# A first mixer whose suffix sums move from TensorE to VectorE, and a packed level of distance 32 in the third

## What is computed

```
log_keep = where(strict, log_sigmoid(-z), 0)
suffix   = reverse cumsum of log_keep over the keys, without the element itself
a        = where(strict, exp(log_sigmoid(z) + suffix), 0)
o        = a @ v
```

## Time and profile before

| | |
|---|---|
| median of 3 runs | 1150.33 us (1150.04 to 1150.42) |
| the profiled execution, its own time | 1150.12 us |
| its span in the trace | 1148.6 us |
| PE busy | 1127.5 us (98%) |
| VectorE busy | 552.2 us (48%) |
| ScalarE busy | 251.0 us (22%) |
| GpSimd busy | 21.6 us (2%) |
| mean granted TensorE clock | 0.998 of 2.4 GHz |

### The profile page before, as it was taken

How to read it: one execution, slowest core, us unless ns; L and a number is a source line. 1 busy time by engine, 2 the same in 40 slices (tenths; PEclk the granted TensorE clock), 3 DMA queues, 4 the chain that set the end, 5 groups by cost and what they waited for, 6 DMA issues and landing times.

```text
span 1148.6 us, 13943 instructions
## 1 busy us (share of the span) xinstructions
PE 1127.5 (98%) x5717; PEld 965.0 (84%) x5717; DVE 552.2 (48%) x1084; ACT 251.0 (22%) x470; POOL 21.6 (2%) x83
## 2 busy tenths in 40 slices
PE   7899999999999999999999999999999999999997
PEld 5688888888888877888888888888889888888886
DVE  2455646455465658553646546567463341221123
ACT  3322223000000045663300000007333410000001
POOL 1000230000000000000000000000000000000000
PEclk9999999999999999999999999999999999999999
DMA  9899718787886762380878688664341544353521
GB/s 350 275 368 323 251 50 311 276 311 245 312 279 243 224 74 74 107 259 2 312 279 301 233 313 284 240 235 130 130 142 41 165 147 147 128 198 114 168 89 37
DMA packets 154592, 234.54 MB, mean 204 GB/s; under 512 B 8817, under 2 KB 126625, under 8 KB 154529
## 3 DMA queue, kind: packets, MB, share of 16 engines
q1 hardware_dynamic: 154172, 233.54, 60.1%
q10 hardware_dynamic: 357, 0.12, 0.0%
HBM read 232.19 MB, written 1.44 MB: 203 GB/s over the span
## 4 chain that ended last, share of the span: by engine, by line
PE 93%; DVE 3%; SPq 1%; ACT 1%; DMA 1%; issue 0%; DVEq 0%
PE PS L687 48%; PE PS L764 20%; PE PS L715 7%; PE PS L700 4%; PE PS L884 2%; PE PS L1164 1%; PE PS L917 1%; DMA ada_slot<-in_ada_w 1%; PE PS L1241 1%; DVE ada_acc L1669 1%; PE PS L608 1%; SPq L384 1%; DVE work L2001 1%; PE PS L900 1%; SPq L375 1%; PE PS L1106 1%
## 5 line engine op out<-in xcount | busy, mean ns | idle before, releaser
L687 PE MATMUL PS<-hT,slot 128*128 128x256 f32 x2672 | 589.7, 379 | 0.8 <-ACT hT L1345 0.8
L687 PEld LDWEIGHTS PS<-hT,slot 128*128 128x128 f32 x2672 | 506.6, 190 | 70.2 <-issue 2.0
L764 PE MATMUL PS<-act,slot 128*128 128x256 f32 x1056 | 238.7, 379 | 0.0
L764 PEld LDWEIGHTS PS<-act,slot 128*128 128x128 f32 x1056 | 200.1, 190 | 28.9 <-issue 1.6
L1797 DVE TENSOR_SCALAR ffn_work<-PS,pcol 128x256 f32<-128x256 f32 x100 | 50.7, 541 | 314.5 <-PE PS L687 314.4
L1380 ACT ACTIVATE ffn_work<-ffn_work 128x256 f32<-128x256 f32 x66 | 27.6, 418 | 612.5 <-DVE ffn_work L1807 612.5
L1669 DVE SCALAR_TENSOR_TENSOR ada_acc<-ada_slot,cond,ada_acc 128x1024 f32<-128x1024 f32 x119 | 152.5, 1282 | 5.2 <-DMA ada_slot<-in_ada_w 0.5
L715 PE MATMUL PS<-oT,slot 128*128 128x256 f32 x384 | 85.1, 380 | 0.0
L715 PEld LDWEIGHTS PS<-oT,slot 128*128 128x128 f32 x384 | 72.2, 190 | 10.4 <-issue 0.9
L700 PE MATMUL PS<-xg,slot 128*128 128x257 f32 (+1 forms) x256 | 57.6, 381 | 0.0
L700 PEld LDWEIGHTS PS<-xg,slot 128*128 128x128 f32 (+1 forms) x256 | 47.7, 187 | 8.1 <-issue 0.8
(11 more groups left out here) (291 smaller groups left out, 758.9 us busy)
## 6 DMA issues: line engine op xcount, KB each, us to landing
ada_slot<-in_ada_w SPq DMA_DIRECT2D x144, 512.0 KB, 8.1
slot<-in_ffn_w_up SPq DMA_DIRECT2D x44, 1024.0 KB, 11.5
slot<-in_ffn_w_down SPq DMA_DIRECT2D x22, 1024.0 KB, 4.9
slot<-in_w_up SPq DMA_DIRECT2D x22, 1024.0 KB, 5.1
slot<-in_sb_w_in SPq DMA_DIRECT2D x11, 1024.0 KB, 12.6
slot<-in_w_in SPq DMA_DIRECT2D x11, 1024.0 KB, 5.2
slot<-in_w_down SPq DMA_DIRECT2D x11, 1024.0 KB, 4.9
slot<-in_dsa_w_in SPq DMA_DIRECT2D x10, 1024.0 KB, 5.3
```

The lines of the kernel that those rows point to most:

```text
L687: last = mm(PS[:, bank, half * T:half * T + T], slot[s][:, k, m * P:(m + 1) * P], x[:, k, :], start=k == 0, stop=k == KC - 1)
L764: last = mm(PS[:, c // 2, (c % 2) * T:(c % 2) * T + T], w[:, j_odd * D + c * P:j_odd * D + (c + 1) * P], act[:, j_odd, :], start=start and ...
```

## The change

In the first mixer the scores are made the other way round (queries x keys: qT stationary, kT moving), so that the sums over later keys run along the free dimension. The two mask products a pair go: VectorE's clamp becomes one `scalar_tensor_tensor` (minimum with 40, then add of `causal`, now strict in the first mixer and rebuilt for the second by GpSimd once `log_ready[1]` has reached 4). The suffix products go: VectorE runs one `tensor_tensor_scan` a pair over 768 reversed elements, with a tile `restart` whose zeros begin each segment, and subtracts; ScalarE takes Exp, PE transposes the weights back (`sb_turn`, six 128 x 128 transposes a pair), ScalarE copies them to `prob`. PE's order becomes scores, query, key, turn, turn, value, mix; in group 3 scores, 36 records of the out projection, turn, 12 records, turn, mix. `mods(2, 0)` moves from the end of group 1 into group 2, between key and turn; the small transposes move into the middle of the value projection. VectorE's first two `ada` steps of each group now stand ahead of the scans, three behind them.

In the third mixer the level of distance 32 is packed: the key halves and the query halves are stored apart, a product takes 64 columns of either, writes 64 partitions in two strips of 32 columns, and two plain copies (`take_quarters`) replace the masked copy.

```diff
+        restart = sb("restart", [P, 2 * 384 + 4])
+        ones = restart[:, 2 * 384 + 4 - P:2 * 384 + 4]
...
+            step(pool.memset(restart[:, :], 1.0))
+            step(pool.memset(restart[:, 0:2 * 384].rearrange("p (e n) -> p e n", e=2)[:, :, 0:384:T], 0.0))
...
+            masked_above(True).then_inc(consts_ready, 1)
...
+            pool.wait_ge(log_ready[1], 4)
+            masked_above(False).then_inc(causal_ready, 1)
...
             def sb_key(i):
                 arrived(sb_slot(i, 1))
                 fill(1)
-                project(2, sb_slot(i, 1), 0, hT)
+                project(2, sb_slot(i, 1), 0, hT, first_frees=sb_slot(i, 0))
...
-                    for lo_t, hi_t, lo_k in ((0, T, 0), (T, T + P, P)):
+                    for lo, hi, tt in ((0, P, 0), (P, 384, 1)):
                         for e in range(2):
-                            b, lo = 4 + 2 * m + e, 64 * e
-                            last = mm(PS[:, b, lo_t:hi_t], kT[lo:lo + 64, m, lo_k:lo_k + P], qT[lo:lo + 64, m, lo_k:T],
-                                      start=lo_k == 0, stop=False, skip_group_check=True)
+                            b, c = 4 + 2 * m + e, 64 * e
+                            last = mm(PS[:, b, lo:hi], qT[c:c + 64, m, tt * P:(tt + 1) * P], kT[c:c + 64, m, 0:hi - lo],
+                                      start=tt == 0, stop=tt == 1, skip_group_check=True)
...
-                    for e in range(2):
-                        b = 4 + 2 * m + e
-                        diagonal = PS[:, b, :].rearrange("p (x t) -> p x t", x=4)[:, 0:3:2, :]
-                        last = mm(diagonal, ident_b[:, :], strict_b[:, :].unsqueeze(1).to_broadcast([P, 2, P]),
-                                  start=False, stop=True, skip_group_check=True)
...
+            def sb_turn(m):
+
+                fill(2 + m)
+                pe.wait_ge(weight_ready[m], bk(f"weight_ready{m}").next())
+                for e in range(2):
+                    for n in range(3):
+                        last = pe.transpose(PS[:, 4 + 2 * m + e, n * P:(n + 1) * P], esp[:, 2 * m + e, n * P:(n + 1) * P],
+                                            ident[:, :])
+                last.then_inc(unit_full[2 + m], 1)
...
             for i in range(4):
                 sb_scores(i)
                 if i < 3:
+                    sb_query(i + 1)
+                    sb_key(i + 1)
                     if i == 2:
-                        mods_taken()
-                    sb_query(i + 1)
+                        was_read(0)
+                        mods(2, 0)
+                    sb_turn(0)
+                    sb_turn(1)
+                    sb_value(i + 1, between=small_columns if i == 2 else None)
+                    sb_mix()
                 else:
                     out_start(0, 0, 6)
...
+                    out_start(0, 1, 6, blocks=(0,))
+                    sb_turn(0)
+                    out_products(0, 1, range(6), blocks=(1,))
+                    sb_turn(1)
                     sb_mix(2)
                     out_start(0, 2, 6)
...
+                        if size == P // 4:
+                            found = PS[0:2 * size, 2 * u + tt, h * P:(h + 1) * P].rearrange("p (b w) -> p b w", w=2 * size)
+                            packed = decayed[n][:, :].rearrange("p (s x w) -> p s x w", s=2, w=2 * size)
+                            last = mm(found[:, :, size:2 * size], packed[:, 0, 2 * h + tt, :], packed[:, 1, 2 * h + tt, :],
+                                      start=True, stop=True)
+                            continue
...
+                    act_e.wait_ge(unit_read[2 + m], bk(f"unit_full{2 + m}").value())
+                    last = act_e.activation(prob[:, 2 * m:2 * m + 2, :], esp[:, 2 * m:2 * m + 2, :], ACT.Exp)
...
                 for m in range(2):
+                    act_e.wait_ge(log_ready[m], bk(f"log_weight{m}").next())
+                    buf = esp[:, 2 * m:2 * m + 2, :]
+                    act_e.activation(buf, buf, ACT.Exp).then_inc(weight_ready[m], 1)
+                for m in range(2):
                     full(2 + m)
-                    act_e.activation(prob[:, 2 * m:2 * m + 2, :], PS[:, 4 + 2 * m:6 + 2 * m, 0:384], ACT.Exp)\
+                    act_e.activation(prob[:, 2 * m:2 * m + 2, :], PS[:, 4 + 2 * m:6 + 2 * m, 0:384], ACT.Copy)\
                         .then_inc(unit_read[2 + m], 1)
...
-                    dve.tensor_scalar(esp[:, 2 * m:2 * m + 2, :], PS[:, 4 + 2 * m:6 + 2 * m, 0:384], 40.0, None, ALU.min)\
-                        .then_inc(z_ready[m], 1)
-                if i == 3:
-                    ada(0, 5, range(0, 2))
+                    dve.scalar_tensor_tensor(esp[:, 2 * m:2 * m + 2, :], PS[:, 4 + 2 * m:6 + 2 * m, 0:384], 40.0,
+                                             causal.unsqueeze(1).to_broadcast([P, 2, 384]), ALU.min, ALU.add)\
+                        .then_inc(unit_read[2 + m], 1)
+                ada(0, i + 2, range(0, 2))
                 for m in range(2):
+                    z, sp = (x[:, 2 * m:2 * m + 2, :].rearrange("p e n -> p (e n)") for x in (esp, prob))
                     dve.wait_ge(e_ready[m], bk(f"log1p_ready{m}").next())
-                    buf = esp[:, 2 * m:2 * m + 2, :]
-                    dve.tensor_tensor(buf, PS[:, 4 + 2 * m:6 + 2 * m, 0:384], buf, ALU.max).then_inc(unit_read[2 + m], 1)
+                    link(dve.tensor_tensor_scan(sp[:, ::-1], restart[:, 0:2 * 384], sp[:, ::-1], 0.0, ALU.mult, ALU.add))
+                    dve.tensor_tensor(z, z, sp, ALU.subtract).then_inc(log_ready[m], 1)
                     skip(2 + m)
+                ada(0, i + 2, range(2, 5))
...
+            def take_quarters(u):
+
+                full(u)
+                w = P // 4
+                found = PS[:, 2 * u:2 * u + 2, :].rearrange("p b (h t) -> p (b h) t", t=P)
+                kept = score.rearrange("p (x t) -> p x t", t=P)
+                link(dve.tensor_copy(kept[0:w, :, w:2 * w], found[0:w, :, w:2 * w]))
+                dve.tensor_copy(kept[2 * w:3 * w, :, 3 * w:P], found[w:2 * w, :, 3 * w:P]).then_inc(unit_read[u], 1)
+                dve.wait_ge(unit_read[u], bk(f"unit_full{u}").value())
```

More of the change, by code:

```diff
@@ L242, in build @@
         act_used = [sem(f"act_used{b}") for b in range(2)]
-        z_ready = [sem(f"z_clamped{m}") for m in range(2)]
+        log_ready = [sem(f"log_weight{m}") for m in range(2)]
+        weight_ready = [sem(f"weight_ready{m}") for m in range(2)]
         e_ready = [sem(f"log1p_ready{m}") for m in range(2)]
@@ L536, in _, with masked_above @@
             step(pool.memset(eps_col[:, :], EPS))
[L537 to L549, removed]
+            def masked_above(first):
+                step(pool.memset(causal, 0.0))
+                for lo in (0, T):
+                    last = pool.affine_select(out=causal[:, lo:lo + P], in_=causal[:, lo:lo + P],
+                                              compare_op=ALU.is_gt if first else ALU.is_ge, fill=NEG,
+                                              base=0, pattern=[[-1, P]], channel_multiplier=1)
+                return last
+            masked_above(True).then_inc(consts_ready, 1)
             pool.wait_ge(rel_cols_ready, 1)
@@ L708, in second, with out_products @@
                 return 1 if n and OUT_UNITS[l][n - 1] == OUT_UNITS[l][n] else 0
-            def out_products(l, n, chunks, frees=None):
+            def out_products(l, n, chunks, frees=None, blocks=(0, 1)):
                 half = second(l, n)
-                for m in range(2):
+                for m in blocks:
                     for k in chunks:
@@ L726, in out_start @@
                     fill(OUT_UNITS[l][n])
-                out_products(l, n, range(chunks), frees=frees)
+                out_products(l, n, range(chunks), frees=frees, blocks=blocks)
             def out_projection(l, started=(), after=None):
@@ L872, in sb_key, with small_columns, sb_value @@
                 fill(1)
-                project(2, sb_slot(i, 1), 0, hT)
+                project(2, sb_slot(i, 1), 0, hT, first_frees=sb_slot(i, 0))
                 project(3, sb_slot(i, 1), 1, hT).then_inc(unit_full[1], 1)
-            def sb_value(i):
+            def small_columns():
+                pe.wait_ge(small_loaded, 16 * N_SMALL_DMAS)
+                mods_taken()
+                fill(0)
+                for t in range(2, NROW):
+                    n = tile_rows[t]
+                    pe.transpose(PS[:, (t - 2) // 4, (t - 2) % 4 * P:(t - 2) % 4 * P + n], prow[0:n, t, :],
+                                 ident[0:n, 0:n])
+                pe.transpose(PS[0:H, 1, 384:384 + NBUCKET], rel_rows[:, :], ident[0:NBUCKET, 0:NBUCKET])\
+                    .then_inc(unit_full[0], 1)
+            def sb_value(i, between=None):
                 s = sb_slot(i, 2)
@@ L887, in sb_value @@
                             last.then_inc(slot_used[sb_slot(i, 1)], 1)
+                    if tt == 0 and between is not None:
+                        between()
```

(26 more changed lines are left out.)

51 lines of the change are left out of this document (16 added, 35 removed).

## The result

| | before | after |
|---|---|---|
| median | 1150.32 us | 1139.64 us (1139.22 to 1140.08, 4 runs) |
| ratio | | 0.9906, interval 0.9894 to 0.9918 |
| the profiled execution | 1150.12 us | 1139.9 us |
| its span | 1148.6 us | 1138.3 us |
| mean granted clock | 0.998 | 0.996 |

The kernel is 0.9% faster; 1139.1 was forecast, in a range of 1137.8 to 1142.5.

A forecast was written before the change was run, and what follows sets the result against it. PE was taken to bound the first mixer. Groups 0 to 2 (8.1), group 3 (2.1) and the third mixer (0.9) sum to 11.1 us saved, giving 1139.1 us, in a range of 1137.8 to 1142.5.

The forecast's parts named there:

- PE bound: First mixer: PE is busy throughout, so each PE microsecond removed is won unless another engine makes PE wait.
- Suffix out, transposes in: Each first-mixer group: suffix sums leave PE, 3.48 us; twelve transposes come in, 1.31 us.
- Masks: Each first-mixer group: the two mask pairs leave PE, 0.54 us won, bounds 0.43 and 0.64; scores unchanged.
- Groups 0 to 2: First mixer: each of these groups wins 2.7 us, together 8.1; moved modulation work and small transposes keep their PE time.
- Group 3: First mixer's last group: 2.1 us won, after PE waits of 0.4 at the first turn and 0.25 at the mix.
- The scan: VectorE, first mixer: a scan of 768 reversed elements takes 1.75 us, between 0.96 and 3.5.
- The cover in groups 0 to 2: The key projection hides the scan chain, 5.6 and 3.6 us spare; without it each group would wait 1.3 us.
- The rival with the doubled scan: Scan takes 3.5 us; groups 0 to 2 hide it, group 3 waits; saved 8.1, 1142.2 us; chance 0.12.
- The slower rival: Scan chain bounds all groups; whole gain gone at a 4.55 us scan, 1154.0 us at 5; chance 0.03.
- Loads: DMA for ada pieces and slabs: group 0's chain 1.1 us late, inside 3.6 spare; everywhere later, loads land in time.
- Third mixer: Level 32 packed: sixteen records take 0.93 us instead of 1.84, 0.9 us won.
- The clock: Rival: PE falls to 1.2 GHz at the transpose bursts, leaving 0.7 us of gain, 1149.6 us; chance 0.02.

The follow-up runs named there:

- e7: The changed kernel with the bfloat16 mask products put back on PE, VectorE still adding its mask too; 1141.13 us.
- e6: The changed kernel with the two turns moved ahead of the key projection in groups 0 to 2; 1155.69 us, ratio 1.0043.
- e8: The changed kernel with the scan's operands not reversed; one run, 1139.82 us.
- e5: The changed kernel with each scan made twice, the first into an unused tile; 1154.03 us, ratio to the kernel before 1.003.
- e10: The changed kernel with some of group 3's out-projection records moved from between the turns to between second turn and mix; 1138.56 us.
- e9: The changed kernel with each scan made twice and three ada steps moved behind the kT copy in groups 0 to 2; 1143.68 us, ratio 0.9942.
- e2: The changed kernel with the third mixer's level 32 unpacked as before, so the first mixer's change alone; 1139.83 us, ratio 0.9909.

## Why the prediction was right, point by point

- **PE bound.** Right. The 10.7 us that the first mixer's stretch lost are PE work less the waits in group 3.
- **Suffix out, transposes in.** 3.48 and 1.31 us forecast; the chain has 3.47 and 1.31. Right, to 0.01.
- **Masks.** Forecast 0.54 us a group, measured 0.65 (e7), at its upper bound of 0.64: the term was mis-sized, by 0.1. The step that failed is that "the scores keep their column counts, 0.85 us a pair; nothing". Both pairs together now take 1.51: 0.85 for the first, behind the mix, and 0.66 for the second, directly behind a like set. With the masks back between them (e7) each takes 0.85 to 0.86 again. In return the query projection, now directly behind the scores, takes 7.10 instead of 6.91 (14.01 less 6.91; 7.12 in e6, where it stands alone in the chain), where 0.1 was kept for the change of shape. Before, scores and masks took twice 0.85 + 0.32 = 2.34; together 2.34 - 1.51 - 0.19 = 0.64, which is e7's 0.65.
- **Groups 0 to 2.** 2.7 us each forecast; 3.01 measured in groups 0 and 1 (28.2 less 25.19). Of the other 0.3, 0.1 is in the masks; 0.2 is in the value projection, 7.10 before and 6.91 now: it stood behind the mix (64 columns), and stands behind transposes (128 columns). The prediction had moved it at no price. Group 2 won only 2.6 (28.70 and the 1.00 us of `mods(2, 0)` before, 27.09 after). There the turns stand behind `mods(2, 0)` and take 1.46 us instead of 1.31, and the value projection, split by the small transposes, takes 3.46 + 3.65 = 7.11. The prediction's "their PE time stays" left out what stands behind the moved work. The sums are by the chain's rows; no run takes these 0.2 us apart.
- **Group 3.** 2.1 forecast, 2.09 measured, which is in part luck: its parts are off both ways. The suffix products took 3.64 us there (3.48 was taken from group 1) and the masks' term was 0.1 more than forecast; but the two turns took 0.85 + 0.67 = 1.52 instead of 1.31, and the mix lost 0.3 where 0.25 was forecast. The first turn began at M+9.86 (139.22 less 129.36) where M+10.0 was forecast, and PE waited 0.4, as forecast.
- **The scan.** 1.75 us forecast from eight short scans, 1.752 measured, and reversal free (e8). The 0.05 us for a start-up was a guess that no row had; by the two lengths it comes to just that (six times 0.33 less 1.75, over five). The Trainium skill's page DVE: opcode table, instruction layouts, handler registers and perf-mode slots (feedback) has the scan at half throughput. The rows agree: 1.75 us for 768 elements, where the subtraction of as many takes 0.96.
- **The cover in groups 0 to 2.** Right that PE doesn't wait, wrong in how much is spare. "Groups 0 to 2 still hide it" failed in e5: the prediction looked at the turned weights alone and not at what else VectorE's queue carries to PE. The kT copy ends at 93.33 us and is wanted at 93.91, so 0.6 us were spare, not 3.6 (row below). The rival with the doubled scan read 1142.2 and set the range's upper end; e5 measured 1154.03. The slower rival had the whole gain gone at a scan of 4.55 us; in e5 it was gone at 3.5. That the scan came out at 1.75 kept this error out of the forecast. "Each group would wait 1.3 us" without the key projection's cover failed in e6 for the same kind of reason: 2.9, by ScalarE's queue.

```profile
92.64 0.69 DVE L1904 COPY kT<-PS 128x512 f32<-128x512 f32 x1
```

- **Loads.** Right that nothing waits. In group 0 the first scan started at 57.87 us, 5.98 behind the first scores, no later than in group 1 (83.21, 6.13 behind). In e10, where the first scores began as early as the prediction had them (50.37), it started at 56.77, 6.40 behind them: about 0.3 us late and not the 1.1 of the prediction.
- **Third mixer.** 0.9 forecast; 0.85 in the stretch.
- **The clock.** No fall at the transposes: the stretch of group 1's turns and all of 52 to 160 us stand at 1.00. The page TensorE: Matmul & The Clock Gate (PE-mode transpose) of the Trainium skill says that the full clock doesn't engage for transposes. Nothing of it shows in bursts of 1.31 us between products; a long run of transposes is in no run here.
- **The sum.** 11.1 us forecast for the profiled execution; 11.7 us by the stretches without the start, 10.3 with it, since that execution lost 1.4 us to the clock at the start. That it came within 1 us of its forecast is thus two errors of opposite sign: the first mixer won 0.5 more, and the start cost 1.4. The prediction had looked for a fall of the clock only around the transposes.

## What to carry to other kernels

When an engine takes over work, list everything that it hands to the bottleneck and not only the result of the new work: here the thinnest margin (0.6 us) was a plain copy behind the scans and three `ada` steps, and moving it forward took 10 us off the kernel with doubled scans, whose work stayed the same. Price a wait of the bottleneck above its length: behind six of the eight pauses of 1.9 to 2.9 us in e5, e6 and e9 PE ran part of the next work at half clock. And read the cost of a product of another shape from what stands behind it too.

## What was not expected of the hardware

- A 64-row set of score products costs 0.66 us when a like set stands ahead of it and 0.85 to 0.86 when a 128-row product does; 32 records of projection cost 6.91 us behind transposes or masks and 7.10 behind the 64-column mix or the 64-row scores.
- The granted clock fell to 0.50 behind some pauses of PE and not behind like ones in the same execution: in e5 behind 2.67 us (group 0) and 2.20 (group 3), not behind 2.85 (group 1) and 1.86 (group 2).
- A stretch can run slow where the table of stretches shows 1.00: the forty products at 12 us in e2 took 4.12 us, against 2.37 in the kernel before.
- A turn of six transposes takes 0.67 us in a stream and 0.85 directly behind a wait.
